# Branch C's projections spread between the attention units of the dilated heads

## The chip, the cores and the metric

The kernel runs on one core of one Trainium2 chip. The metric is the time of one execution in microseconds on the device. The kernel before takes 1748.67 us (median of 3 runs, 1744.22 to 1750.66). Engines are named as in the profile: PE is TensorE (PEld its weight loads), DVE is VectorE, ACT is ScalarE, POOL is GpSimd, SP is the engine that only issues DMAs here. All data is float32.

## The reference, cut to what matters

One layer for 512 prompt tokens and 8 x 8 sample tokens. The part that the change touches is the mixer:

```python
z = jnp.einsum('bld,de->ble', h, w_in)      # D_MODEL 1024
u, qb, kb, vb, qc, kc, vc, gl = jnp.split(z, cuts, axis=-1)
for g, (win, dil) in enumerate(((128, 1), (512, 4), (2048, 16))):
    o_g, l_g = dilated_prompt(qb[:, :, g], kb[:, :, g], vb[:, :, g], dil, bias_b[g])
oc, _ = band_attn(qc, kc, vc, bias_c, SWA_WINDOW, sink)   # branch C: 8 heads, 2 kv heads, 64 wide
y = merge(a, ob, lse, oc, gl, w_b_up, w_c_up, w_out)
```

`u` feeds the pooling branch, `qb, kb, vb` the 12 dilated heads (branch B), `qc, kc, vc` the 8 window heads (branch C). The dilated heads need nothing of branch C's projections. After the prompt's attention come the sample tokens' attention over cached keys, the merge, and the mixture of 64 experts, none of which is touched.

## The kernel before, in words

All engines run a fixed program, with semaphores between them. PE's results go through eight PSUM banks of 512 columns. A list of "fills", written by `plan()`, says in which order PE fills banks, which bank each fill takes (a ring over the banks), and whether ACT ("A") or DVE ("D") empties it. Before a fill PE waits until the fill that had its bank last has been emptied (`bank_for`). Each engine takes its work strictly in the order of its own code.

The projections: `by_channel` computes 128 channels x 288 tokens in 8 accumulated matmuls (`KD` = 8), `by_token` 128 tokens x 256 channels in 8. The order is u, q 0 to 5, k, v (branch B), and then branch C: q 6 to 9 in two halves each (8 fills of 8 matmuls with 288 moving columns) and kvc 0 to 4 (5 fills of 8 with 256). Two small fills `uout` (the last pooling rows, sent out by SP) follow, then the keys are turned: `kT` 0 to 6 (4 transposes each; 6 is branch C's key) and `kTs` (7 transposes of the sample tokens' keys).

Then the prompt's attention, 40 units in `UNITS`: 8 of the head group 1, 8 of group 2, 8 of group 0, 16 of branch C. A unit is two heads on one block of 128 queries. Units run in a software pipeline of 43 steps `s`: in step s PE makes the scores S of unit s (two matmuls; 128 columns each for the groups 1 and 2 and the first blocks, 256 for the others), turns the probabilities T of unit s - 2 (2 or 4 transposes), and multiplies with the values, O, for unit s - 3 (2 or 4 matmuls of 128 columns). For unit s DVE adds the bias and takes the maximum (L1700, L1704), ACT takes the exponential (L1274) and empties T (L1184), and DVE writes the outputs of unit s - 3 (L1652 to L1654). Queries of the groups 1 and 2 are read with a stride of four floats, as the stationary operand: `q = qT[rows, cq, t:SEQ:4]`.

Two waits stand in the pipeline. ACT waits before step 0 for `u_out`, the two DMAs of the pooling rows, whose staging place the scores take over. DVE waits at step 3 (`if s == LAGO`) for `kv_out`, all 28 DMAs that send keys and values out, because its `stage` array lies on the keys `kTM`. When the groups 1 and 2 are staged, SP writes them to `fold` in HBM and reads them back in token order; POOL and DVE combine the groups at step 30, and PE turns the result (`bT`) at step 37.

SP issues its DMAs in the order of its code: after the weights the bias tables, `u_out`, the keys and values out, then four loads of cached keys into the slots 3, 0, 1 and 2, then `fold`. A slot is 4096 floats per partition; a load waits until the slot's last reader on PE is done (`LAST`). POOL issues copies of the caches from HBM to HBM, one after each of the fills in `COPY_AT`.

Of the kernel before, what the change touches and what calls it, by code (L numbers as in the profile page):

```python
# [17 lines left out]
ACT = mybir.ActivationFunctionType  # L18
# [3 lines left out]
P = 128  # L22
# [37 lines left out]
def plan():  # L60
# [36 lines left out]
    for c in range(6, 10):  # L97
        for h in range(2):
            fill(("q", c, h), "AD"[h])
    for t in range(TILES):  # L100
        fill(("kvc", t), "AD"[t % 2])
    fill(("uout", 0), "A")
    fill(("uout", 1), "A")
    for m in range(7):
        fill(("kT", m), "AD"[m % 2])
    fill(("kTs",), "D")
# [94 lines left out]
LAGT, LAGO = 2, 3  # L201
COMBINE_AT = 27
# [151 lines left out]
def build(nc, x_prompt, x_sample, cache_b1, cache_b2, cache_b3, cache_c, state_pool, c_prompt, c_sample,  # L354
# [13 lines left out]
    with ExitStack() as ctx:  # L368
# [87 lines left out]
        stage = at(A_KTM, 3, PT_ * 264)  # L456
# [237 lines left out]
        def _(sp):  # L694
# [156 lines left out]
            for t in range(TILES):  # L851
# [3 lines left out]
                wait_emptied(sp, ("kvc", t))  # L855
                for kv, src in ((0, kTM), (1, vTM)):
# [4 lines left out]
                    if t == PT_ - 1:  # L861
                        sp.dma_start(b1_p[0, 0, :, kv, :, :].rearrange("i h d -> i (h d)"),
                                     src[:, t, 0:256]).then_inc(kv_out, 16)
                        sp.dma_start(c_p[0, 0, :, kv, :, :].rearrange("i h d -> i (h d)"),
                                     src[:, t, 768:896]).then_inc(kv_out, 16)
                    if t == PT_:

                        for o, n, w, c in [(outs_s[g], CACHE[g], 256, 256 * g) for g in range(3)] + [(c_s, P, 128, 768)]:
# [4 lines left out]
            for key in kload[:4]:  # L873
                load(key)
# [7 lines left out]
            for g in (1, 2):  # L882
                sp.dma_start(stage[:, g, :].rearrange("p (t c) -> p t c", t=PT_),
                             fold[g - 1].rearrange("(t p) c -> p t c", p=P)).then_inc(stage_in, 16)

# [286 lines left out]
        def _(act):  # L1172
# [61 lines left out]
            for c in range(6, 10):  # L1234

                bank = wait_fill(act, ("q", c, 0))
                for e in range(2):
                    h = 2 * (c - 6) + e
                    ins = act.activation(qT[64 * (h // 4):64 * (h // 4) + 64, 6 + h % 4, 0:288],
                                         bank[64 * e:64 * e + 64, 0:288], ACT.Copy)  # L1240
                ins.then_inc(emptied["A"], 1)
            for t in range(0, TILES, 2):
                r = parts(t)
                bank = wait_fill(act, ("kvc", t))
# [1492 lines left out]
```

## Time and profile before

| | us |
|---|---|
| median of 3 runs | 1748.67 (1744.22 to 1750.66) |
| the profiled execution | 1733.79, its span 1732.1 |
| PE busy | 1563.6 (90% of the span) |
| ACT busy | 509.6 |
| DVE busy | 474.7 |
| POOL busy | 264.9 |
| granted TensorE clock, mean | 0.928 |

A clock of 1.00 is 2.4 GHz, and 0.50 is 1.2 GHz. A float32 matmul of the program stands in the trace as two records of PE. Records overlap in the pipeline, so a record's mean duration is longer than the distance between starts; distances between starts, and busy time divided by the count, are the ones to add up. A PE that is busy by the trace is not PE at its peak.

### The profile page before, as it was taken

How to read it: one execution, taken by the hardware profiler on the slowest of the kernel's cores; microseconds unless marked ns; L12 is line 12 of the kernel's file. 1: busy time of each engine (PE TensorE's matmuls, PEld its weight loads, DVE VectorE, ACT ScalarE, POOL GpSimd, SP SyncE). 2: the span in 40 equal slices, each digit the busy share in tenths (PEclk: the TensorE clock that was granted, in tenths of full speed). 3: DMA queues.
4: the chain of work that ended last, by engine and by line, in shares of the span. 5: the costliest groups of instructions: out<-in, count | busy, mean ns of one | idle time of the engine just before them, and what ended most of it. 6: DMA issues, size and time to landing. Idle time of an engine off the chain costs nothing.

```text
span 1732.1 us, 22957 instructions
## 1 busy us (share of the span) xinstructions
PE 1563.6 (90%) x7181; PEld 881.1 (51%) x7182; DVE 474.7 (27%) x953; ACT 509.6 (29%) x854; POOL 264.9 (15%) x322
## 2 busy tenths in 40 slices
PE   4489999989897999997889879999999999999955
PEld 1057888877764777775345423333333333333311
DVE  2030000145672111111266422222222222212137
ACT  2110000045641000000233234444454444444321
POOL 0030051000300000000111112212122221211153
PEclk7689999966997999998989989999999999999988
DMA  8892379472388936549534299999879998999867
GB/s 289 302 337 26 50 235 331 163 241 64 131 279 257 302 94 203 178 160 329 207 123 169 85 364 393 345 383 411 325 275 342 405 420 341 420 417 422 321 266 249
DMA packets 140516, 461.29 MB, mean 266 GB/s; under 512 B 13401, under 2 KB 78425, under 8 KB 111308
## 3 DMA queue, kind: packets, MB, share of 16 engines
q1 hardware_dynamic: 117853, 331.36, 52.3%
q0 software_dynamic: 22608, 129.18, 21.1%
q8 instruction: 36, 0.59, 0.1%
q14 instruction: 19, 0.16, 0.0%
HBM read 424.80 MB, written 109.28 MB: 308 GB/s over the span
## 4 chain that ended last, share of the span: by engine, by line
PE 79%; DMA 7%; DVE 3%; SPq 3%; POOL 2%; issue 2%; ACT 2%; another core or an unknown queue 1%; ACTq 0%; POOLq 0%; DVEq 0%
PE bank L2107 72%; PE bank L2639 3%; POOL arena L1166 2%; DMA arena<-in_we_down 2%; SPq L783 1%; PE bank L2272 1%; DMA arena<-in_cache_b 1%; PE bank L2661 1%; PE bank L2313 1%; DMA arena<-in_w_in 1%; DMA arena<-in_w_ada 1%; DMA mods<-arena 1%; DMA arena<-in_we_gate 1%; DMA pscale<-in_pool_scale 1%
## 5 line engine op out<-in xcount | busy, mean ns | idle before, releaser
L2107 PE MATMUL bank<-arena 128*64 (+10 forms) x6096 | 1417.0, 513 | 118.4 <-DMA arena<-in_w_ada 26.5
L2107 PEld LDWEIGHTS bank<-arena 128*64 128x64 f32 (+3 forms) x6096 | 748.7, 173 | 680.9 <-issue 467.3
L1184 ACT ACTIVATE arena<-bank 128x512 f32<-128x512 f32 (+6 forms) x152 | 75.1, 505 | 350.5 <-PE bank L2107 219.8
L2026 DVE COPY arena<-bank 128x512 f32<-128x512 f32 x52 | 36.0, 692 | 409.0 <-PE bank L2639 409.0
L1441 ACT ACTIVATE arena<-arena 128x2048 f32 x52 | 99.7, 1918 | 19.5 <-DMA arena<-in_we_gate 15.7
L1128 POOL DMA_INDIRECT arena<-h2rows,icol x54 | 95.6, 1771 | 46.6 <-POOL icol L1124 46.6
L1450 ACT ACTIVATE arena<-arena 128x2048 f32 x52 | 99.3, 1910 | 11.4 <-issue 11.4
L1533 DVE COPY arena<-bank 128x512 f32<-128x512 f32 (+6 forms) x70 | 41.8, 606 | 209.7 <-PE bank L2107 185.8
L1460 ACT ACTIVATE arena<-bank 128x256 f32<-128x256 f32 x52 | 19.9, 383 | 239.5 <-PE bank L2107 239.5
L1323 ACT ACTIVATE arena<-bank 128x288 f32<-128x288 f32 x48 | 19.7, 410 | 233.6 <-PE bank L2107 233.6
L1085 POOL DMA_DIRECT2D out<-in_cache_b x24 | 12.0, 507 | 429.5 <-PE bank L2107 429.5
L2639 PEld LDWEIGHTS bank<-ident,arena 128*128 128x128 f32 x416 | 50.9, 194 | 44.6 <-issue 44.6
L2021 DVE COPY arena<-arena 128x2048 f32 x52 | 63.3, 1218 | 27.2 <-ACTq L1433 27.2
L1124 POOL COPY icol<-arena 128x1 uint32 (+1 forms) x54 | 9.6, 178 | 358.3 <-PE bank L2639 357.7
L2639 PE MATMUL bank<-ident,arena 128*128 128x128 f32 x416 | 60.9, 290 | 2.4 <-issue 2.4
L2041 DVE COPY arena<-bank 128x512 f32<-128x512 f32 x52 | 35.9, 691 | 80.4 <-PE bank L2107 80.4
L1844 DVE SCALAR_TENSOR_TENSOR arena<-bank,pscale,arena 128x288 f32<-128x288 f32 x16 | 8.3, 518 | 167.6 <-PE bank L2107 167.6
L1137 POOL DMA_DIRECT2D yrows<-arena x52 | 30.1, 579 | 131.1 <-DVE arena L2041 110.3
L1471 ACT ACTIVATE arena<-bank 128x512 f32<-128x512 f32 x52 | 31.0, 596 | 61.1 <-PE bank L2107 61.1
L1166 POOL DMA_INDIRECT arena<-yrows,arena x40 | 39.7, 993 | 15.1 <-issue 11.9
L1465 ACT ACTIVATE arena<-bank 128x512 f32<-128x512 f32 x52 | 31.0, 597 | 35.5 <-PE bank L2639 35.5
L2661 PEld LDWEIGHTS bank<-ident,arena 128*128 128x128 f32 x104 | 16.5, 207 | 42.7 <-issue 41.4
(235 smaller groups left out, 732.3 us busy)
## 6 DMA issues: line engine op xcount, KB each, us to landing
arena<-in_we_gate SPq DMA_DIRECT2D x64, 1024.0 KB, 11.2
arena<-in_we_up SPq DMA_DIRECT2D x64, 1024.0 KB, 13.6
arena<-in_we_down SPq DMA_DIRECT2D x64, 1024.0 KB, 11.0
out<-in_cache_b POOLq DMA_DIRECT2D x8, 4080.0 KB, 15.0
yrows<-arena POOLq DMA_DIRECT2D x52, 512.0 KB, 9.2
arena<-in_w_ada SPq DMA_DIRECT2D x12, 2048.0 KB, 16.7
arena<-in_cache_b SPq DMA_DIRECT2D x18, 1024.0 KB, 8.4
arena<-in_w_in SPq DMA_DIRECT2D x7, 2048.0 KB, 15.5
```

What stands on the lines that cost most here:

```text
L1128: pool.indirect_dma_start(xg[:, j, :], None, h2rows, bass.IndirectOffsetOnAxis(ap=icol[:, j:j + 1], axis=0), bounds_check=TOK - 1, oob_is_ ...
L1166: pool.indirect_dma_start(gbuf[n % GBUFS][0:r, :], None, yrows, bass.IndirectOffsetOnAxis(ap=rowi[0:r, TOPK * t + k:TOPK * t + k + 1], axis=0)
L1184: act.activation(out, pick(bank), ACT.Copy).then_inc(emptied["A"], 1)
L1441: act.activation(whalf[:, 2048:4096], arena[:, bass.ds(base + 2048, 2048)], ACT.Copy).then_inc(up_copied, 1)
L1450: act.activation(whalf[:, 4096:6144], arena[:, bass.ds(base + 4096, 2048)], ACT.Copy).then_inc(d_copied, 1)
L1533: dve.tensor_copy(out, pick(bank)).then_inc(emptied["D"], 1)
L2021: dve.tensor_copy(whalf[:, 0:2048], arena[:, bass.ds(base, 2048)]).then_inc(gate_copied, 1)
L2026: dve.tensor_copy(xT[:, 512:1024], psb[2][:, :]).then_inc(xt_dve, 1)
L2041: dve.tensor_copy(yb[:, off % 2, 512:1024], psb[5][:, :]).then_inc(y_dve, 1)
L2107: return pe.matmul(out, lhsT, rhs, start=first, stop=last)
L2639: ins = pe.transpose(psb[1 + k // 4][:, P * (k % 4):P * (k % 4 + 1)], xg[:, off % 2, k:D:KD], ident[:, :])
L2661: ins = pe.transpose(psb[3][:, k * P:(k + 1) * P], act3[:, 1, k:FF:2], ident[:, :])
```

## The change

Branch C's 13 projection fills (8 of q, 5 of kvc) leave their place ahead of `uout`. Their 104 matmuls are dealt out over the steps 0 to 20 of the attention pipeline, five per step: two behind the scores S, two behind the transposes T, one behind the products O. They use the banks 6 and 7 in turn; the other fills of the attention rotate over the banks 0 to 5. ACT empties the even ones, DVE the odd ones, at the same places of their own step. `kT` 6 and `kTs` move to the head of step 22 (`KEYS_AT`), and the first unit of branch C (step 24) waits for them.

`stage` moves from the keys' place to slot 3, so the wait for `kv_out` moves from step 3 to step 27, the first output of branch C. Slot 3's first cached-key load comes after the last `bT` fill, slot 2's after `kvc` 4 and behind `fold`, and branch C's keys and values go out behind `fold` as well.

```diff
+    ring["set"], ring["n"] = list(range(6)), 0
+
+    def between(s, place):
+        for x in beside(s, place):
+            if x % KD == KD - 1:
+                j = x // KD
+                fill(BESIDE[j], "AD"[j % 2], 6 + j % 2)
 
     for s in range(len(UNITS) + LAGO):
+        if s == KEYS_AT:
+            fill(("kT", 6), "A")
+            fill(("kTs",), "D")
         if s < len(UNITS):
             fill(("S", s), "D")
+        between(s, 0)
         if 0 <= s - LAGT < len(UNITS):
             fill(("T", s - LAGT), "A")
+        between(s, 1)
         if 0 <= s - LAGO < len(UNITS):
             fill(("O", s - LAGO), "D")
+        between(s, 2)
...
+BESIDE = [("q", c, h) for c in range(6, 10) for h in range(2)] + [("kvc", t) for t in range(TILES)]
+KEYS_AT = 22
+
+def beside(s, place):
+    lo, hi = ((0, 2), (2, 4), (4, 5))[place]
+    return range(5 * s + lo, min(5 * s + hi, KD * len(BESIDE)))
...
-        stage = at(A_KTM, 3, PT_ * 264)
+        stage = at(3 * SLOT, 3, PT_ * 264)
...
-            for key in kload[:4]:
+            for key in kload[1:3]:
                 load(key)
...
+            for t in (PT_ - 1, PT_):
+                wait_emptied(sp, ("kvc", t))
...
+            load(kload[3])
+            sp.wait_ge(fills_done, INDEX[("bT", PT_ - 1)] + 1)
+            load(kload[0])
...
-                if s == LAGO:
+                if s - LAGO == UNITS.index(("C", 0, 0)):
                     dve.wait_ge(kv_out, 16 * KV_OUTS)
...
+            def between(s, place):
+
+                for x in beside(s, place):
+                    j, k = divmod(x, KD)
+                    key = BESIDE[j]
+                    if k == 0:
+                        bank_for(pe, key)
+                    bank = psb[6 + j % 2]
+                    w = wait_load(pe, ("in", 5 if j < 4 else 6))
+                    if key[0] == "q":
+                        col = 256 + (key[1] - 6) * P if j < 4 else (key[1] - 8) * P
+                        ins = mm(bank[:, 0:288], w[:, 512 * k + col:512 * k + col + P],
+                                 hT[:, k, 288 * key[2]:288 * key[2] + 288], k == 0, k == KD - 1)
+                    else:
+                        ins = mm(bank[0:parts(key[1]), 0:256], hT[:, k, toks(key[1])],
+                                 w[:, 512 * k + 256:512 * k + 512], k == 0, k == KD - 1)
+                    if k == KD - 1:
+                        close(ins)
```

On PE, at the end of the projections and the head of the attention, the program stood as follows before (288 columns are q 6 to 9, 256 kvc, the 15- and 64-row ones `uout`, L2233 `kT`, L2237 `kTs`, then S of the units 0 to 2 and T of unit 0).

```order
L2107 MATMUL bank2<-arena 128x288 x8
L2107 MATMUL bank3<-arena 128x256 x8
...
L2107 MATMUL bank7<-arena 64x256 x8
L2219 MATMUL bank0<-ident,arena 15x128 x4
L2223 MATMUL bank1<-ident,arena 64x128 x4
L2233 MATMUL bank2<-ident,arena 128x128 x4
...
L2233 MATMUL bank0<-ident,arena 128x128 x4
L2237 MATMUL bank1<-ident,arena 128x64 x7
L2107 MATMUL bank2<-arena 128x128 x2
L2107 MATMUL bank3<-arena 128x128 x2
L2107 MATMUL bank4<-arena 128x128 x2
L2272 MATMUL bank5<-ident,arena 128x128 x2
```

The same engine and place now (L2294 is `kT`, L2344 T, L2156 all matmuls; the 288-column ones are q 6).

```order
L2283 MATMUL bank4<-ident,arena 64x128 x4
L2294 MATMUL bank5<-ident,arena 128x128 x4
...
L2294 MATMUL bank2<-ident,arena 128x128 x4
L2156 MATMUL bank0<-arena 128x128 x2
L2156 MATMUL bank6<-arena 128x288 x5
L2156 MATMUL bank1<-arena 128x128 x2
L2156 MATMUL bank6<-arena 128x288 x3
L2156 MATMUL bank7<-arena 128x288 x2
L2156 MATMUL bank2<-arena 128x128 x2
L2156 MATMUL bank7<-arena 128x288 x2
L2344 MATMUL bank3<-ident,arena 128x128 x2
```

Ahead of the first T, PE now has 12 projection matmuls besides the three units' scores. On SP, from the pooling rows to `fold`, the order is now this (L863, L864 the pooling rows, L874 to L882 keys and values out, L744 to L755 cached keys, L892 `fold`).

```order
L863 DMA out_6<-arena 15x512 [waits emptied_by_act]
L864 DMA out_11<-arena 8x8x512
L874 DMA out_3<-arena 128x256 [waits emptied_by_act]
...
L882 DMA out_9<-arena 8x8x256
L744 DMA arena<-in_cache_c 128x8x128 [waits fills_done]
L746 DMA arena<-in_cache_b1 128x8x256
L755 DMA arena<-in_cache_b3 128x8x256 [waits fills_done]
...
L892 DMA fold<-arena 128x264 [waits stage_ready]
```

Two of the four cached-key loads stand ahead of `fold` where all four did, and the other two behind it.

## Rows read from the trace of the kernel before

**Rows 1.** The page: busy time by engine; granted clock in 40 slices.
```profile
PE 1563.6 (90%) x7181; PEld 881.1 (51%) x7182; DVE 474.7 (27%) x953; ACT 509.6 (29%) x854; POOL 264.9 (15%) x322
...
PEclk7689999966997999998989989999999999999988
```

**Rows 2.** Stages from-to: length, busy time (records) of each engine, clock, DMA share, GB/s.
```profile
300.30:348.60 48.30, 48.30 (x209) 38.21 (x208) 4.62 (x12) 4.16 (x13) 0.00 (x0) 1.00 0.50 167
348.60:353.90 5.30, 4.58 (x43) 4.23 (x42) 2.70 (x4) 3.76 (x8) 0.00 (x0) 1.00 0.30 91
...
371.10:413.40 42.30, 42.30 (x149) 33.95 (x150) 21.29 (x79) 18.87 (x79) 0.00 (x0) 0.50 0.61 191
...
484.70:521.20 36.50, 35.87 (x322) 23.48 (x320) 25.96 (x50) 17.74 (x35) 0.00 (x0) 1.00 0.91 289
```

**Rows 3.** The same view in stretches of 5 us, where the clock moves.
```profile
355.00:360.00 5.00, 2.52 (x12) 2.03 (x10) 2.35 (x6) 3.72 (x13) 0.00 (x0) 0.63 0.79 263
...
415.00:420.00 5.00, 5.00 (x27) 4.39 (x28) 2.94 (x7) 2.08 (x6) 0.00 (x0) 0.73 0.41 147
```

**Rows 4.** PE in order of time: start, length, what [idle before, released by].
```profile
353.94 2.10 PE L2107 MATMUL bank<-arena 64*128 64x128 f32 x12 [0.77 <-DVE arena L1533]
358.52 0.66 PE L2272 MATMUL bank<-ident,arena 128*128 128x128 f32 x2 [2.48 <-ACT arena L1274]
...
371.08 0.66 PE L2272 MATMUL bank<-ident,arena 128*128 128x128 f32 x2 [2.58 <-DVE arena L1700]
...
373.75 0.69 PE L2272 MATMUL bank<-ident,arena 128*128 128x128 f32 x2
...
376.45 0.69 PE L2272 MATMUL bank<-ident,arena 128*128 128x128 f32 x2
...
414.91 1.11 PE L2272 MATMUL bank<-ident,arena 128*128 128x128 f32 x4
...
421.27 0.66 PE L2272 MATMUL bank<-ident,arena 128*128 128x128 f32 x4
...
423.39 0.66 PE L2272 MATMUL bank<-ident,arena 128*128 128x128 f32 x4
```

**Rows 5.** Matmul forms on PE, 301 to 349.4 us: records, busy us, mean ns.
```profile
L2107 PE MATMUL bank<-arena 128*128 128x288 f32 x125 | 30.5, 406 | 0.0
L2107 PE MATMUL bank<-arena 128*128 128x256 f32 x64 | 14.0, 379 | 0.0
```

**Rows 6.** The same, 205 to 245 us (stationary operand read with stride 4).
```profile
L2107 PE MATMUL bank<-arena 128*128 128x256 f32 x130 | 31.3, 401 | 0.0
```

**Rows 7.** DVE in order of time, at the wait of step 3.
```profile
368.51 0.17 DVE L1652 COPY arena<-nmx 128x2 f32<-128x2 f32 x1 [7.18 <-PE bank L2107]
```

**Rows 8.** Emptying half of q 6 to 9, 301 to 349 us, on DVE.
```profile
L1622 DVE COPY arena<-bank 64x288 f32<-64x288 f32 x8 | 3.6, 456 | 31.7 <-PE bank L2107 31.6
```

**Rows 9.** SP's and POOL's DMA issues and ACT's first exponential, in order of time.
```profile
350.70 0.71 SPq L848 DMA_DIRECT2D out<-arena  x1
...
406.16 4.75 SPq L879 DMA_DIRECT2D fold<-arena  x8
...
285.42 1.46 POOL L1085 DMA_DIRECT2D out<-in_cache_b  x3 [20.65 <-PE bank L2107]
...
356.20 1.28 ACT L1274 ACT_TABLE_LOAD   x1 [2.97 <-DVE nmx L1704]
```

**Rows 10.** DMA issues, KB each, us to landing: 285 to 326 us, then 200 to 500.
```profile
out<-in_cache_b POOLq DMA_DIRECT2D x1, 1008.0 KB, 39.3
...
arena<-in_cache_b SPq DMA_DIRECT2D x8, 1024.0 KB, 8.4
...
arena<-toep SPq DMA_DIRECT2D x12, 128.0 KB, 4.2
```

**Rows 11.** PE: `bT` and the first cached keys of group 2.
```profile
461.12 1.04 PE L2301 MATMUL bank<-ident,arena 128*128 128x128 f32 x8
...
490.50 1.97 PE L2313 MATMUL bank<-ident,arena 128*128 128x128 f32 x16
```

More of the change, by code:

```diff
@@ L1250, in _ @@
             act.wait_ge(tables_out, 16 * 8)
-            for m in range(0, 7, 2):
+            for m in range(0, 6, 2):
                 empty(("kT", m), kT[:, m, 0:SEQ])
@@ L1256, in _ @@
             for s in range(len(UNITS) + LAGO):
+                if s == KEYS_AT:
+                    empty(("kT", 6), kT[:, 6, 0:SEQ])
+                between(s, 0)
                 u = s - LAGT
@@ L1712, in _ @@
                     outputs(s - LAGO)
+                between(s, 2)
+                if 0 <= s - LAGO < len(UNITS):
                     if s - LAGO == COMBINE_AT:
@@ L2228, in _, with turned_own_keys @@
                     wait_emptied(pe, ("k", g, t))
-                wait_emptied(pe, ("kvc", t))
-            for m in range(7):
+            def turned_own_keys(m):
                 bank = bank_for(pe, ("kT", m))
@@ L2234, in _ @@
                 close(ins)
-            bank = bank_for(pe, ("kTs",))
-            for m in range(7):
-                ins = pe.transpose(bank[:, m * NS:(m + 1) * NS], kTM[0:NS, PT_, m * P:(m + 1) * P], ident[0:NS, 0:NS])
-            close(ins)
-            for m in range(7):
+            for m in range(6):
+                turned_own_keys(m)
+            for m in range(6):
                 wait_emptied(pe, ("kT", m))
@@ L2245, in _ @@
             for h in range(2):
-                wait_emptied(pe, ("q", 9, h))
+                wait_emptied(pe, ("q", 5, h))
             for s in range(len(UNITS) + LAGO):
+                if s == KEYS_AT:
+                    for t in range(TILES):
+                        wait_emptied(pe, ("kvc", t))
+                    turned_own_keys(6)
+                    bank = bank_for(pe, ("kTs",))
+                    for m in range(7):
+                        ins = pe.transpose(bank[:, m * NS:(m + 1) * NS], kTM[0:NS, PT_, m * P:(m + 1) * P],
+                                           ident[0:NS, 0:NS])
+                    close(ins)
                 if s < len(UNITS):
                     kind, t, p = UNITS[s]
+                    if (kind, t, p) == ("C", 0, 0):
+                        wait_emptied(pe, ("kT", 6))
+                        for h in range(2):
+                            wait_emptied(pe, ("q", 9, h))
                     bank = bank_for(pe, ("S", s))
@@ L2263, in _ @@
                     close(ins)
+                between(s, 0)
                 u = s - LAGT
@@ L2275, in _ @@
                     close(ins)
+                between(s, 1)
                 u = s - LAGO
@@ L2290, in _ @@
                     close(ins)
+                between(s, 2)
                 for key in after_unit(u):
```

91 lines of the change are left out of this document (49 added, 42 removed).

## The prediction

> **What bounds the kernel now.** I read the page first. PE is busy for 90% of the span, and its granted clock is low in a few slices [rows 1]. Slices 9 and 10 (346 to 433 us) read 6: the attention of the prompt. The stage view shows why it matters. From 300.3 to 348.6 us PE does branch C's projections at clock 1.00. From 371.1 to 413.4 us it is busy without a break at clock 0.50, while DVE works 21.3 of 42.3 us and ACT 18.9 [rows 2]. So in that stretch neither DVE nor ACT nor a DMA ends last: PE does, at 1.2 GHz. PE in order of time shows steps of 2.70 us (373.75 to 376.45) in the groups 1 and 2, and 2.12 us (421.27 to 423.39) for larger units once the clock is back [rows 4]. The clock fell between 355 and 360 us, when PE idled 0.77 and 2.48 us with a stretch of transposes just before, and rose between 415 and 420 us, when units with 256-column scores came [rows 3, 4]. Since all that follows is chained to the attention's end, a microsecond saved here is one off the span.
>
> **The old interval.** Everything compared lies between 300.3 us (first matmul of q 6) and the scores of step 21. T of step 21 starts at 414.9 [rows 4]; the 512 score columns ahead of it took about 1.7 us at the low clock, so step 21 began near 413.2. Old: 48.3 (projections) + 5.3 (`uout`, keys turned, up to 353.9) + 59.3 (steps 0 to 20) = 112.9 us. In the 59.3 lie two stalls of PE: 2.48 us for the first exponential and 2.58 us for the wait of step 3, at which DVE sat 7.18 us [rows 4, 7].
>
> **The new interval, if PE keeps its full clock.**
> - The 104 matmuls cost the same wherever they stand: 48.3 us. From the forms, two records of 288 columns take 0.488 us (30.5/62.5), that is 1.69 ns per column; of 256, 0.4375 us [rows 5].
> - The units' own work. A full-clock step of 2.12 us holds 1024 matmul columns (1.73 us at 1.69 ns) and 4 transposes, which leaves 0.10 us for each. Steps 0 to 20 hold 6144 columns of scores (18 units of 256, 3 of 512), 4608 of outputs (18 units) and 40 transposes: 10.4 + 7.8 + 3.9 = 22.1 us.
> - Scores of the groups 1 and 2 load a strided stationary operand. The projections that do so took 31.3/130 = 0.241 us a record against 14.0/64 = 0.219 [rows 5, 6], so 0.24 us looks like the price of one such load. A unit has four records: up to 0.96 us against 0.43 for its columns, with the first load behind a projection matmul. I take 0.4 us of excess for each of 16 units, 6.4 us; the ends are 0 and 8.5.
> - `uout` and 24 instead of 28 transposes, with the wait for the last copy: 5.3 less about 0.45 and 0.65 for what moved to step 22: 4.2 us. At step 22 that 1.1 us is paid again, now at the side of units at full clock.
> - DVE's and ACT's added emptying: DVE's halves are 0.456 us each [rows 8], two per fill, 6 fills in 21 steps; with 1.3 us of unit work a step (21.3 us in some 16 steps [rows 2]) DVE is at half of a 3.8 us step. ACT is lighter. Cost nothing; if a step were as short as before the change at full clock, they would show.
> - Stalls: the wait at step 3 is gone. Before the first T, PE now has 12 projection matmuls, 5.9 us, and three units' scores. `u_out` is issued near 302 us, into the shadow of POOL's third cache copy (issued 285.4, 39.3 us to landing, so until 324.7) [rows 9, 10]. Before it had landed within 5 us of its issue at 350.7 to 351.4, as ACT began at 356.2. T of unit 0 needs it by about 310. Small hardware-queue transfers landed in 4.2 us at the median [rows 10]. I take 1 us of stall, ends 0 and 14.
> - The clock's start: `kT` transposes and a gap of about 1 us come before step 0, as before. If it dips there, dense matmuls follow at once; I take 1 us, ends 0 and 4.
>
> New: 48.3 + 22.1 + 6.4 + 4.2 + 1 + 1 = 83.0 us, against 112.9: 29.9 us less. Behind it: the 1.1 us of step 22; six banks instead of eight for the branch C units, where DVE is the busier engine, 1 us (0 to 4); and T of the steps 21 and 22, which ran half slow (415 to 420 us at 0.73 [rows 3]), come at full clock, 2.1 us gained. Net 29.9 - 1.1 - 1 + 2.1 = 29.9, say **30 us**.
>
> What could be late next. `fold` takes 4.75 us to issue [rows 9] and some 4 to land, by the small transfers [rows 10]; then comes 1 us of issue for the read-back, and branch C's outputs, about 2 us to issue and 4 to land: 16 us in all. From step 18 (when it starts) to step 27 (where DVE now waits for `kv_out`) two mixed steps and seven of 2.12 us or more pass, 22 us: covered, with 6 us to spare. Slot 3's keys are now requested after `bT` (461.1), are two loads of 8.4 us to landing, 17 us even one after the other, and group 2's turn begins 29 us later (490.5) [rows 10, 11]: covered.
>
> **A rule weighed.** In the stretch from 484.7 to 521.2 us PE cycles through banks in short groups, many of them of transposes, and the clock stays at 1.00 [rows 2, 11]. The Trainium skill says the opposite of both habits: "TensorE: Matmul & The Clock Gate", section "A second HAM failure mode: psum-queue depth-cycling", has groups that cycle through banks with small gaps throw the clock back and forth, and its section "Part 4: PE-mode transpose" says that transposes do not count as busy. By these rules the half-clock rival below would be likelier than I make it; the trace disagrees once the clock is up, and agrees for 355 to 415 us.
>
> **The rivals.**
> - *The clock stays at 1.2 GHz through the mixed steps* (slower). PE in order cannot shed the added matmuls, so each costs double: 96.6 us, and the units what they cost before less the stalls, 59.3 - 5.1 = 54.2. With 4.2: 155.0 against 112.9, and 2.1 us behind: 44 us slower, **1793 us**. For it: 42 us of unbroken PE work at 0.50 did not lift the clock [rows 2]. Against it: a mixed step is two thirds full-height matmuls of 256 and 288 columns, which ran at 1.00 for the whole of 300 to 348 us, and thinner steps lifted it at 415 to 420 us. It decides from about 8 of the 21 steps on: a step at half clock costs some 3.7 us more, and the gain is 30.
> - *The units keep their 2.70 us* because the hand-over S, DVE, ACT, T, O sets it, and the projections only add: 48.3 + 54.2 + 4.2 = 106.7, 6 us less, with 2 behind 4: **1745 us**. Against it: DVE and ACT idle half the time in the old steps, and two steps lie between S and T.
> - *The new wait is `u_out`*: it lands only when the cache copy is through, at 324.7. PE stands for 14 us from about 310, and some 3 us more go into a cold clock: 30 - 17 + 1 + 1 = 15 us gained, **1734 us**. Against it: the bias tables, small and on the same hardware queue, landed in 4.2 us beside other loads [rows 10].
>
> The Trainium skill, "DMA: Bandwidth & Descriptors", section "Queues, rings and completion order", has each DMA engine take turns between its queues, packet by packet; by that, the third rival would not come.
>
> **How the numbers follow.** The trace is of an execution of 1733.8 us (span 1732.1 and 1.7 around it), 14.9 us under the median; 30 us off it are 1703.8, and off the median **1719 us**. I expect the median's offset to stay. The ends of the costs give a gain of 39 (no strided excess, no stall) to 20: 1710 to 1729 us; with the 3 us by which the three runs spread, 1706 to 1732. Chances: forecast 0.76, `u_out` 0.08, units' period 0.07, half clock 0.07, anything else 0.02. Up to 1736 the range holds the `u_out` rival too, and leaves out about 0.17. About 0.5% (9 us) is what can be told from no change here: faster by more is 0.86, within it 0.06, slower by more 0.08.
>
> **What would show it.** Right: clock 1.00 from 305 us to the end of the mixed steps; steps of 3.5 to 4 us, PE busy throughout; step 21 begins near 383; no idle time of DVE at step 3. Wrong: a clock of 0.50 beyond the first two or three steps; PE idle ahead of the first T with ACT waiting for the pooling rows; PE idle in the mixed steps, released by DVE or ACT; DVE standing at step 27; or PE waiting for slot 3's keys.

## The result, and the profile after

Beside the kernel before (1748.67 us) the changed kernel has a median of 1735.09 us over five executions (1730.67 to 1738.24): ratio 0.9922, 95% interval 0.99 to 0.9944, so 13.6 us faster (9.8 to 17.5), where 30 were forecast. Timed again later beside the kernel before (e13 below) it had 1737.85 against 1747.10, ratio 0.9961 (0.9935 to 0.9988). The mechanism came as forecast; its size was less than half.

The page after, busy time and granted clock as in [rows 1]:

```profile
PE 1560.6 (90%) x7181; PEld 873.6 (50%) x7182; DVE 476.3 (27%) x953; ACT 508.9 (29%) x854; POOL 268.3 (15%) x322
...
PEclk8589999999897999998989789999999999999987
```

Slices 9 and 10, which read 6, now read 9. PE's work is the same; it is done at the higher clock. By stages, with the columns of [rows 2] (from-to: length, busy time and records of PE, PEld, DVE, ACT, POOL, then clock, DMA share, GB/s): `uout` and keys; first scores to first T; T of unit 0 to T of unit 19 (made in step 21); and four stretches of 2 us in which the clock falls:

```profile
303.40:308.30 4.90, 3.64 (x34) 3.39 (x33) 2.08 (x3) 3.11 (x6) 0.00 (x0) 1.00 1.13 386
308.30:322.40 14.10, 11.50 (x36) 8.42 (x37) 2.53 (x6) 2.31 (x6) 0.00 (x0) 0.88 0.97 336
322.40:403.60 81.20, 81.20 (x373) 61.19 (x373) 29.37 (x102) 27.59 (x113) 0.00 (x0) 0.98 0.41 133
...
310.00:312.00 2.00, 2.00 (x6) 1.39 (x5) 0.45 (x2) 1.28 (x1) 0.00 (x0) 0.50 1.00 331
312.00:314.00 2.00, 2.00 (x7) 1.33 (x6) 0.00 (x0) 0.00 (x0) 0.00 (x0) 0.80 0.37 135
324.00:326.00 2.00, 2.00 (x6) 1.09 (x6) 0.00 (x0) 0.91 (x5) 0.00 (x0) 0.50 0.79 265
326.00:328.00 2.00, 2.00 (x10) 1.51 (x10) 1.34 (x4) 0.00 (x1) 0.00 (x0) 0.89 1.41 433
```

The stage of mixed steps is what the forecast wanted: busy 81.20 of 81.20 us, clock 0.98, DVE and ACT each at about a third. The clock dips twice, each time for some 3 us. PE in order of time (start, length, what, [idle before, released by]), which answers to [rows 4]:

```profile
303.37 0.61 PE L2279 MATMUL bank<-ident,arena 128*15 128x128 f32 x4
...
308.30 11.50 PE L2156 MATMUL bank<-arena 64*128 64x128 f32 x36 [1.26 <-DVE arena L1569]
322.40 0.41 PE L2344 MATMUL bank<-ident,arena 128*128 128x128 f32 x2 [2.60 <-ACT arena L1309]
322.65 5.09 PE L2156 MATMUL bank<-arena 128*128 128x288 f32 x14
...
336.41 0.38 PE L2344 MATMUL bank<-ident,arena 128*128 128x128 f32 x2
336.63 4.36 PE L2156 MATMUL bank<-arena 128*128 128x288 f32 x18
340.83 0.38 PE L2344 MATMUL bank<-ident,arena 128*128 128x128 f32 x2
...
403.56 0.66 PE L2344 MATMUL bank<-ident,arena 128*128 128x128 f32 x4
```

A mixed step takes 4.42 us (336.41 to 340.83). The T of step 21 (unit 19) stands at 403.56, before at 414.91 [rows 4]: the lead in this pair of traces is 11.4 us. The same view of SP and ACT shows what PE waited 2.60 us for:

```profile
305.17 0.37 SPq L863 DMA_DIRECT2D out<-arena  x1
305.58 0.70 SPq L864 DMA_DIRECT2D out<-arena  x1
306.53 24.34 SPq L874 DMA_DIRECT2D out<-arena  x10
...
310.56 1.28 ACT L1309 ACT_TABLE_LOAD   x1 [3.32 <-DVE nmx L1749]
321.38 0.40 ACT L1309 ACTIVATE arena<-arena,nmx 128x128 f32<-128x128 f32 x1 [9.54 <-DMA out<-arena]
```

SP issues the two writes of the pooling rows (`u_out`) by 306.28. ACT has its table at 311.8 and then stands until 321.38, released by those writes: 15 us from issue to landing. Before, with the issue at 350.70 to 351.41, ACT did not wait for them: its table load began at 356.20 [rows 9]. In the changed kernel this wait stands ahead of the first T.

Matmul forms on PE, 327 to 371 us (ten steps), which answer to [rows 5]:

```profile
L2156 PE MATMUL bank<-arena 128*128 128x288 f32 x98 | 29.6, 417 | 0.0
L2156 PE MATMUL bank<-arena 64*128 64x128 f32 x40 | 12.0, 419 | 0.0
L2156 PE MATMUL bank<-arena 128*128 128x128 f32 x40 | 6.1, 274 | 0.0
L2344 PE MATMUL bank<-ident,arena 128*128 128x128 f32 x20 | 3.8, 273 | 0.0
```

A unit has four records of scores (64 rows) and four of outputs (128 rows), of the same 128 columns. The outputs are busy 6.1 us, the scores 12.0. Here most of the forecast's error lies; a part of the difference, the strided read, it had in its sum.

### The profile page after: what moved, and what is told of

It reads as the page before. It is cut to its first block, busy times and chain, and to the rows that moved or that the text cites. A ratio compares the mean times of both kernels' runs of the same rounds, so it can differ in the third digit from the quotient of the medians.

```text
span 1733.5 us, 22973 instructions
## 1 busy us (share of the span) xinstructions
PE 1560.6 (90%) x7181; PEld 873.6 (50%) x7182; DVE 476.3 (27%) x953; ACT 508.9 (29%) x854; POOL 268.3 (15%) x322
## 4 chain that ended last, share of the span: by engine, by line
PE 78%; DMA 9%; DVE 3%; SPq 3%; issue 2%; ACT 2%; POOL 1%; another core or an unknown queue 1%; ACTq 0%; DVEq 0%; POOLq 0%
PE bank L2156 72%; PE bank L2713 3%; DMA arena<-in_we_down 3%; DMA arena<-in_w_ada 2%; SPq L799 1%; DMA arena<-in_cache_b 1%; DMA arena<-yrows,arena 1%; PE bank L2387 1%; POOL arena L1190 1%; PE bank L2735 1%; DMA out<-arena 1%; DMA mods<-arena 1%; PE bank L2344 1%; DMA pscale<-in_pool_scale 1%
## 5 line engine op out<-in xcount | busy, mean ns | idle before, releaser
L2156 PE MATMUL bank<-arena 128*64 (+11 forms) x6096 | 1420.4, 513 | 124.8 <-DMA arena<-in_w_ada 24.9
L2156 PEld LDWEIGHTS bank<-arena 128*64 128x64 f32 (+3 forms) x6096 | 741.6, 172 | 694.7 <-issue 478.5
L1486 ACT ACTIVATE arena<-arena 128x2048 f32 x52 | 99.3, 1910 | 11.4 <-issue 11.4
## 6 DMA issues: line engine op xcount, KB each, us to landing
arena<-in_we_down SPq DMA_DIRECT2D x64, 1024.0 KB, 11.4
```

The source lines that it names most:

```text
L1486: act.activation(whalf[:, 4096:6144], arena[:, bass.ds(base + 4096, 2048)], ACT.Copy).then_inc(d_copied, 1)
L2156: return pe.matmul(out, lhsT, rhs, start=first, stop=last)
```

## The experiments

Where a time is compared with another trace, the stretch meant is from the first scores (S of step 0) to T of unit 19, which step 21 makes: 95.3 us in the trace after, 96.4 in its second one (e13). The recorded expectations call its end "T of step 19".

| run | edit against the changed kernel | median us (executions) | ratio to before beside it (95%) | mixed step, us |
|---|---|---|---|---|
| e2, e16 | pooling rows staged elsewhere | 1723.50 (6), 1728.80 (4) | 0.9882 (0.9837-0.9928), 0.9883 (0.9817-0.9949) | 4.42 |
| e3 | scores read contiguously | 1725.21 (6) | 0.9885 (0.984-0.9931) | 3.93 |
| e4 | five projection matmuls in a row | 1729.86 (9) | 0.9916 (0.9891-0.9941) | 4.41 |
| e5 | nothing spread | 1747.28 (10) | 1.0019 (0.9994-1.0043) | 2.70, pure |
| e6 | e5 and e2 | 1743.64 (10) | 0.9993 (0.9964-1.0021) | 2.70, pure |
| e7 | e2, only two groups spread | 1727.24 (6) | 0.9892 (0.986-0.9924) | see text |
| e8 | e2, queries folded when emptied | 1717.50 (6) | 0.9848 (0.9819-0.9877) | 3.93 |
| e9 | e8, scores over 128 rows | 1710.04 (4) | 0.9807 (0.9771-0.9843) | 3.54 |
| e10 | fourth cache copy late | 1723.48 (4) | 0.9878 (0.983-0.9925) | 4.42 |
| e12 | e2, three matmuls a step | 1729.81 (6) | 0.9899 (0.9864-0.9934) | 3.28 |
| e13 | none | 1737.85 (12) | 0.9961 (0.9935-0.9988) | 4.42 |
| e14, e15 | two cache copies late | 1722.90 (4), 1728.68 (6) | 0.9861 (0.9809-0.9913), 0.9894 (0.9837-0.9952) | 4.42 |

**e1_before**: the kernel before, traced again.

> The kernel before, traced once more on the chip of the other runs. The traces before and after have nearly the same span (1732.1 and 1733.5 us), though the medians differ by 13.6 us. Theory A (the trace of before was a favourable execution: its granted clock happened to stay high from 920 to 990 us and at 465 us): this span comes out at 1742 to 1750 us, with less clock in stretches after the attention. Theory B (profiled executions of before are always faster than timed ones): again 1730 to 1735 us.

1738.61 us, span 1736.9: between the two ranges. Its steps are again 2.70 us and its stalls 2.48 and 2.55 us, so the stretch at half clock is a property of the kernel; the executions of the kernel before that were timed in that session lie between 1730.97 and 1753.76. A single execution says nothing about 10 us.

**e2_uout** and **e16_uout_again**: the rows wait elsewhere to be written out, and ACT no longer waits for them.

```diff
-        uouts = at(A_SC + 2 * UE + 4 * NS, 2, 512)
+        uouts = at(3072, 2, 512)
...
+            sp.wait_ge(u_out, 16 * U_OUTS)
             for key in [k for k in kload[4:5]] + [("V", "c0", 0)] + kload[5:]:
...
-            act.wait_ge(u_out, 16 * U_OUTS)
```

> The kernel after, with the pooling rows staged at the end of slot 0, where nothing is written until SP loads the second cached-key block, so ACT no longer waits for their two DMAs before the first exponential. Theory A (ACT's wait for u_out until 321 us cost PE the 2.6 us of idling, and the clock a second fall at 322 to 326 us): first exponential near 311 us, no idle time of PE before the first T, and 3 to 5 us off the kernel after (1730 us). Theory B (the clock falls anyway at the gap of 1.3 us before step 0, and PE ran slowly until 313): PE's idling goes, but the time to step 3 shrinks by 2.6 us or less.

> The changed kernel with the pooling rows staged elsewhere, so that ACT doesn't wait for their landing, timed and traced again beside the same kernel before. First it had 1723.5 us (ratio 0.9882) and 89.7 us from the first scores to T of step 19. Theory A: 1719 to 1727 us, ratio 0.984 to 0.989. Theory B: 1730 to 1735 us, ratio 0.990 to 0.993. Both expect no idle PE at the first T and 89 to 91 us.

PE in order of time, e2:

```profile
306.55 9.83 PE L2156 MATMUL bank<-arena 64*128 64x128 f32 x36 [1.29 <-DVE arena L1569]
316.22 0.38 PE L2344 MATMUL bank<-ident,arena 128*128 128x128 f32 x2
...
320.19 0.38 PE L2344 MATMUL bank<-ident,arena 128*128 128x128 f32 x2
```

No idle time before the first T, which comes 9.67 us after the first scores instead of 14.1, and the first step takes 3.97 instead of 5.18 us. The stretch is 89.6 us in both traces, 5.6 less than after. e16's median (1728.80) lies between the ranges of its two theories, its ratio (0.9883) in the first's; the ten executions have a mean of 1725.0 us.

**e3_nostride**: the scores of the groups 1 and 2 read contiguous query columns (the wrong tokens; the same amount of work).

```diff
-                        q = qT[rows, cq, t:SEQ:4] if kind in (1, 2) else qT[rows, cq, toks(t)]
+                        q = qT[rows, cq, toks(t)]
```

> The kernel after, with the queries of the groups 1 and 2 read as 128 neighbouring tokens instead of every fourth (the scores of these groups are then those of other queries). Mixed steps took 4.42 us against a forecast of 3.84. Theory A (the strided stationary operand costs 0.5 us a step, as the two units of group 0 with 128 columns suggest: 3.66 against 4.15 us): steps of 3.9 us, 16 x 0.5 = 8 us off. Theory B (the step is long because of the hand-overs between small groups): steps of 4.3 us or more.

PE in order of time, e3:

```profile
330.06 0.38 PE L2344 MATMUL bank<-ident,arena 128*128 128x128 f32 x2
330.28 3.87 PE L2156 MATMUL bank<-arena 128*128 128x288 f32 x18
333.99 0.38 PE L2344 MATMUL bank<-ident,arena 128*128 128x128 f32 x2
```

3.93 us a step: the strided load costs 0.49 us a unit. In this trace PE stood 9.31 us ahead of the first T, again released by ACT: the wait for the pooling rows varies.

**e4_grouped**: the five projection matmuls of a step in one place.

```diff
-    lo, hi = ((0, 2), (2, 4), (4, 5))[place]
+    lo, hi = ((0, 5), (5, 5), (5, 5))[place]
```

> The kernel after, with all five projection matmuls of a step behind the scores, instead of two, two and one behind S, T and O. Theory A (each change between a unit's short matmuls and the projections exposes a weight load of about 0.15 us): 4 changes a step fewer, steps of 4.42 - 0.4 = 4.0 us, 6 to 8 us off. Theory B (only the strided loads cost): steps stay at 4.4 us.

4.41 us a step against 4.42: taking the projections in one place instead of three saves nothing. The first theory fell; the 0.4 us too many in every step had to come from the units' own matmuls. From T of unit 1 to T of unit 19 it took 73.7 us against 76.0. Three matmuls (1.4 us) more stand ahead of that stretch here; the other 0.9 us falls in the last group's steps. Its stationary operand is 64 columns wide, and in the changed kernel it changes form at each of its places; that this change is the cause is argued, not shown.

**e5_none** and **e6_uout_none**: all thirteen groups of branch C ahead of `uout`, as before, in the banks 6 and 7, and all else as in the changed kernel; e6 adds e2's edit.

```diff
+NPRE = 13
...
+    if s < 0:
+        return range(KD * NPRE)
...
+            between(-1, 0)
```

> The kernel after with all 13 projection fills back ahead of the pooling rows (still in the banks 6 and 7); stage in slot 3, the moved waits, six banks and the late keys stay. It is the change without the spreading. Theory A (the spreading gives the gain, by the clock): the clock falls before the first T as before, steps of 2.70 us, no wait at step 3, so 3 to 5 us off the kernel before and 6 to 12 us slower than the change. Theory B (the moved wait gives most of it): as fast as the change, about 1733 us.

> As e5, and the pooling rows staged in slot 0 as in e2, so that neither stall is left. Theory A (the clock falls in any gap behind transposes, and PE still waits 2.5 us for the first exponential's table load): clock 0.50 from before step 2, steps of 2.70 us. Theory B (the two stalls brought the clock down): clock 1.00 throughout, steps of about 2.0 us, 12 us or more off e5.

PE in order of time, e5:

```profile
359.76 0.66 PE L2355 MATMUL bank<-ident,arena 128*128 128x128 f32 x2 [2.48 <-ACT arena L1318]
...
364.29 0.69 PE L2355 MATMUL bank<-ident,arena 128*128 128x128 f32 x2
364.77 2.29 PE L2166 MATMUL bank<-arena 128*128 128x128 f32 x8
366.99 0.69 PE L2355 MATMUL bank<-ident,arena 128*128 128x128 f32 x2
```

PE in order of time, and by stages, e6:

```profile
360.49 0.66 PE L2355 MATMUL bank<-ident,arena 128*128 128x128 f32 x2 [1.14 <-ACT arena L1318]
...
360.00:370.00 10.00, 9.51 (x35) 7.87 (x36) 4.79 (x18) 5.74 (x26) 0.00 (x0) 0.50 0.59 182
```

The stall at step 3 is gone, the wait for `kv_out` is later, the bank split is the new one, and nothing is gained (ratio 1.0019 and 0.9993), not even the 3 to 5 us that the first theory gave to the moved wait: the steps stand at 2.70 us again. The gain is the spreading alone. In e6 PE is idle for only 1.26 us ahead of the first scores and 1.14 ahead of the first T, and the clock is at 0.50 from 360 us on all the same. As these two short stalls remain, e6 shows that shorter stalls don't keep the clock, and not what happens with none.

**e7_uout_few2** and **e11_few2_again** (the same kernel): e2, with eleven groups ahead and the last two spread over the steps 0 to 3 (the lines are against e6's kernel).

```diff
-NPRE = 13
+NPRE = 11
```

> As e2, but only the last two fills (16 matmuls) are spread, over the steps 0 to 3; eleven stand ahead. Theory A (the clock needs something to keep it only across the first gap; the old steps were long only by the clock): clock 1.00 up to step 21 with steps of 1.9 to 2.1 us in the groups 1 and 2 (0.87 us of columns, 0.2 of transposes, 0.5 for the stride, some 0.4 of exposed weight loads), total within 3 us of e2. Theory B (thin steps let the clock fall by themselves): it falls after step 3 and steps are 2.70 us again, 15 us slower than e2.

> The kernel of e7 traced once more: its traced execution took 1749.8 us and the others 1715 to 1734. Theory A (where the thin steps lose the clock is chance): the clock falls at another step or not at all, and the span is 10 us or more shorter. Theory B (the thin steps lose it at the same place each time): 0.50 from step 6 again and about 1745 us.

PE in order of time, e7:

```profile
362.14 0.44 PE L2355 MATMUL bank<-ident,arena 128*128 128x128 f32 x2
...
364.08 0.44 PE L2355 MATMUL bank<-ident,arena 128*128 128x128 f32 x2
...
366.03 0.63 PE L2355 MATMUL bank<-ident,arena 128*128 128x128 f32 x2
...
368.67 0.69 PE L2355 MATMUL bank<-ident,arena 128*128 128x128 f32 x2
```

And its clock in stretches:

```profile
360.00:365.00 5.00, 5.00 (x26) 3.75 (x24) 2.05 (x7) 2.15 (x10) 0.00 (x0) 1.00 0.68 198
365.00:370.00 5.00, 5.00 (x20) 4.34 (x20) 2.56 (x11) 2.61 (x12) 0.00 (x0) 0.61 1.10 355
370.00:375.00 5.00, 5.00 (x20) 4.19 (x20) 2.50 (x10) 1.89 (x10) 0.00 (x0) 0.50 0.70 224
```

A pure step at full clock takes 1.94 us. In this trace the clock falls to 0.50 after the last mixed step although PE hasn't been idle for an instant, and the step becomes 2.70 us; e11's trace does the same at the same place (clock 0.61 at 370 to 375 us). So in these two executions, of 1749.76 and 1746.72 us, the pure steps lost the clock without a stall.

They are the two longest of this kernel's seven, and the others speak against making a rule of them. The five that weren't traced took 1715.45 to 1734.07 us, with a mean of 1725.8 and a mean clock over the whole execution of 0.933 to 0.944. The ten of e2 and e16, with all thirteen groups spread, have a mean of 1725.0 us and a clock of 0.937 to 0.946; e6's ten, with none spread, 1744.1 us and 0.918 to 0.929. Two groups over four steps thus gave the time that thirteen gave, as the first theory said of the total. That the clock held in those five is likely by these numbers, but no trace shows it. Whether the pure steps or the stalls ahead of them cost the old kernel its clock stays open.

**e8_foldq_uout**: e2, and the queries of the groups 1 and 2 are written in folded order when their banks are emptied, so that all scores are read contiguously. This computes all of the reference.

```diff
+                    empty(("q", c, 0), qT[:, c, 0:SEQ].rearrange("p (r i) -> p i r", r=4)[:, 0:72, :],
+                          lambda b: b[:, 0:288].rearrange("p (i r) -> p i r", r=4))
...
-                        q = qT[rows, cq, t:SEQ:4] if kind in (1, 2) else qT[rows, cq, toks(t)]
+                        q = qT[rows, cq, toks(t)]
```

> As e2, and the queries of the groups 1 and 2 are written in folded order when their banks are emptied (strided writes on ACT and DVE, one more DVE copy for each of four fills), so the scores read them without a stride. It computes all of the reference. Theory A (the stride costs 0.49 us a step, the writes are hidden behind PE): mixed steps of 3.93 us, 7.8 us off e2, about 1716 us. Theory B (the strided writes make ACT or DVE late in the projections): PE idle during q 2 to 5.

The step is 3.93 us, as in e3, and the emptying with a stride costs nothing that shows. At 1717.50 us (1718.0 in the mean, against 1725.0 of e2 and e16) it is the fastest kernel that does the whole work, 26 us under the kernel before beside it.

**e9_fullheight**: e8, and the scores contract over all 128 rows instead of one head's 64. Each score is then the sum of two heads, so this kernel doesn't compute the reference; it only prices the height.

```diff
-                        rows = slice(half, half + 64)
+                        rows = slice(0, P)
```

> As e8, but the scores take all 128 rows of queries and keys instead of the 64 of their head (each score is then the sum of two heads). Same columns, same number of weight loads. In e8's mixed step of 3.93 us the single records show 0.10 us extra before and 0.10 behind the first record at each change from a 128-row operand to a 64-row one and back, 0.39 us in all. Theory A (the change of height costs 0.2 us each way, because the next weights aren't loaded ahead): steps of 3.54 us, and 16 us less over the 40 units where PE is what ends last. Theory B (it is the semaphore wait ahead of the scores that holds the load back): steps stay at 3.9 us.

PE in order of time, e9:

```profile
329.47 0.38 PE L2354 MATMUL bank<-ident,arena 128*128 128x128 f32 x2
329.69 3.48 PE L2166 MATMUL bank<-arena 128*128 128x288 f32 x18
333.01 0.38 PE L2354 MATMUL bank<-ident,arena 128*128 128x128 f32 x2
...
391.62 0.60 PE L2354 MATMUL bank<-ident,arena 128*128 128x128 f32 x4
392.05 1.50 PE L2166 MATMUL bank<-arena 128*128 128x128 f32 x12
393.39 0.38 PE L2354 MATMUL bank<-ident,arena 128*128 128x128 f32 x2
```

With as many records and columns the step falls from 3.93 to 3.54 us, and a later pure step from 2.12 to 1.77. The 0.39 us is the price of going from 128 rows to 64 and back; the wait for a semaphore ahead of the scores is still there, so the second theory fell. The whole gained less than the 16 us expected: the mean of the executions fell from 1718.0 to 1711.3 us. In the single records of the trace after, the load ahead of a unit's first scores starts 385 ns after the load before it has ended, and the first full-height record behind them takes 0.35 us to the next start instead of 0.24: about 0.2 us each way. The Trainium skill ("TensorE: Matmul & The Clock Gate", section "Step-by-step: what each phase is for") says that a load is pulled ahead of matmuls in flight where the row groups don't conflict or where it goes to the background weight buffer, and that its time goes by the columns and not by the rows. Within one height the trace agrees: records of 128 columns start every 0.11 us. At each change of height the load wasn't ahead; which of the page's two conditions was missing there no run shows.

**e10_copy_late**, **e14_two_copies_late** and **e15_two_late_again**: POOL's fourth cache copy put off; then the third and the fourth.

```diff
-        COPY_AT = [("k", 0, 0), ("k", 2, 0), ("v", 0, 0), ("v", 2, 0), ("S", 30), ...
+        COPY_AT = [("k", 0, 0), ("k", 2, 0), ("S", 12), ("S", 20), ("S", 30), ...
```

> The kernel after, with POOL's fourth cache copy started after the scores of unit 16 instead of after the first value fill of group 2. Theory A (the pooling rows' DMAs landed 15 us after their issue because that copy filled the DMA engines): ACT's wait for them ends within 5 us of the issue, no idle time of PE before the first T, as in e2. Theory B (they are late for another reason, as SP's own queue): ACT waits until about 321 us again.

> The changed kernel with the third and the fourth cache copy of POOL put off: issued when the scores of the steps 12 and 20 are done, instead of when a value projection of group 0 and one of group 2 are. With the fourth alone put off the pooling rows, issued at 305.0 to 306.2 us, still landed only at 320.3, ACT standing 8.6 us. Theory A, these small writes wait behind the copies under way, three of which were issued together at 263 to 270 us: with two copies only, they land within 5 us of their issue, ACT's first exponential follows its table load (about 312 us), the first T comes at 313 to 314 us without an idle PE, the clock stays 1.00, and the time is 3 to 6 us under the changed kernel's. Theory B, the copies aren't it (it is the queue of SP's own transfers, or the form of the writes): ACT waits until about 320 us as before, no gain. The put-off copies run beside other work; on their account I expect nothing.

> The kernel with two cache copies put off, timed and traced again. In its one trace T of step 19 comes 3.9 us earlier after the first projection of branch C's successor stage than in the changed kernel's two traces (first scores to T of step 19: 91.3 us against 95.3 and 96.4), yet four executions have a median 15 us under the changed kernel's in the same session (1722.9 against 1737.9). Theory A, the 15 us are real: median 1719 to 1727 us and ratio 0.984 to 0.989 again, and a trace of an execution at that time shows a second stretch, outside 300 to 420 us, where it is shorter than the changed kernel's by some 10 us. Theory B, four executions are few: median 1730 to 1735 us, ratio 0.990 to 0.993, 4 us under the changed kernel.

ACT in order of time, e10 and then e14:

```profile
320.32 0.40 ACT L1309 ACTIVATE arena<-arena,nmx 128x128 f32<-128x128 f32 x1 [8.61 <-DMA out<-arena]
```

```profile
310.64 1.28 ACT L1309 ACT_TABLE_LOAD   x1 [3.33 <-DVE nmx L1749]
311.93 0.40 ACT L1309 ACTIVATE arena<-arena,nmx 128x128 f32<-128x128 f32 x1
```

SP in order of time, e14:

```profile
305.65 0.70 SPq L864 DMA_DIRECT2D out<-arena  x1
306.61 8.52 SPq L874 DMA_DIRECT2D out<-arena  x14
```

With the fourth copy alone put off, ACT still waited for the rows until 320.3. With the third put off too, they had landed when ACT's table was there, 5.6 us after the last issue, PE had no idle time at the first T, and SP needed 8.5 us to issue fourteen key and value writes where it had needed 24.3 for ten. So it is the cache copies under way, but not the one that my rival named (issued at 288.94 in the trace after, at 285.42 before [rows 9]).

The landing times in the traces say which. The copies land one after another: in the trace after the first three, issued from 262.80 to 267.90, had wholly landed at 282.0, 299.5 and 318.5 us, the fourth at 334.4. ACT went on at 321.38, behind the third and well ahead of the fourth; in e13 at 320.72 (third copy 319.7), in e10 at 320.32 (320.1). e3 fits less well (third 313.5, fourth 330.0, ACT 324.09). In e14 the last copy under way had landed at 291.8, ahead of the rows' issue, so there the rows met no copy at all.

e14's clock dipped even so (0.68 at 308 to 312 us), e15's didn't; the stretch took 91.3 and 89.6 us. e15's median and ratio lie between what its two theories said, and its trace has no other stretch that is 10 us shorter. The ten executions of the two have a mean of 1726.1 us.

**e12_rate3**: e2, with six groups ahead and seven spread at three matmuls a step.

```diff
+NPRE = 6
...
-    lo, hi = ((0, 2), (2, 4), (4, 5))[place]
+    lo, hi = ((0, 1), (1, 2), (2, 3))[place]
```

> As e2, but six fills stand ahead and the other seven are spread at three matmuls a step, over the steps 0 to 18. By e7 and e2 a unit's step costs 1.95 us at full clock and a projection matmul 0.49 on top, wherever it stands. Theory A (three matmuls a step still keep the clock): steps of 1.95 + 1.46 = 3.41 us at clock 1.00, total within 3 us of e2. Theory B (a step must be more than half projections): the clock falls, steps of about 5.6 us.

Clock by stretches, e12:

```profile
330.00:335.00 5.00, 5.00 (x15) 3.51 (x15) 1.15 (x3) 0.88 (x4) 0.00 (x0) 0.64 0.88 300
335.00:340.00 5.00, 5.00 (x16) 3.34 (x16) 1.38 (x4) 0.98 (x5) 0.00 (x0) 0.68 0.58 184
...
350.00:385.00 35.00, 35.00 (x173) 28.17 (x171) 15.30 (x60) 13.25 (x59) 0.00 (x0) 1.00 0.11 36
```

In this trace three matmuls a step hold the clock as well as five do, after a dip at the start: 3.28 to 3.45 us a step, where 3.41 was expected.

**e13_after_again**: the changed kernel, timed and traced again.

> The changed kernel, timed again in five rounds beside the kernel before, and traced again. Open is how much of the miss (30 us forecast, 13.6 measured) lies in the steps and how much is scatter of the executions. Theory A, a part is scatter: from the first 288-column matmul to the first scores of the sample units the two traces of before took 369.6 and 372.6 us, the trace of the changed kernel 353.1, so 18 us less; and two near relatives of it (fourth copy late, projections grouped) were timed at 1723.5 and 1729.9 beside a before of 1744. Then the ratio comes out at 0.988 to 0.991, 1723 to 1728 us, a gain of 16 to 21 us, and the stretch takes 353 us again. Theory B, the 13.6 us are what it gives: ratio 0.992 to 0.995, 1730 to 1735 us. Either way the trace shows steps of 4.42 us and ACT waiting until about 321 us for the pooling rows.

Neither theory: the gain beside the kernel before is 6.8 us (2.1 to 11.4) by the ratio, less than both. All 17 executions of the changed kernel have a mean of 1738.1 us (standard error 1.1), 78 of the kernel before in the later sessions 1745.0 (0.6): 7 us. The 13.6 us of the first comparison rest on five executions of each: the median of before was 3.7 us above that mean, the changed kernel's 3.0 below its own. The trace of e13 has the same steps, and ACT waited until 320.72; PE stood 3.26 us at the first T. But from the first 288-column matmul to the sample units' first scores it took 359.9 us, not 353 again.

## Why the prediction was wrong

**What held.** The old interval was read rightly: 42 us at half clock, bound by PE (e1 shows it again, e5 brings back its steps). The clock came to 1.00 in the mixed steps and stayed; the projection matmuls cost what they did (single records start every 0.243 us, as 30.5 us over 125 records said [rows 5]) and added to the units' work; PE never stood in the mixed steps; DVE's stall at step 3 went; no wait came at step 27 or for slot 3's keys. The rivals of half clock and of the units' own period were rightly low.

**The step that failed is the new interval, in its terms for the units.** From `uout` to the start of step 21 the forecast had 83.0 us; the trace has 99.3 (303.37 to about 402.7, as T at 403.56). The 16.3 us too many, by runs (in each row the excess is measured less forecast):

| term | forecast | measured | from |
|---|---|---|---|
| 64-row scores beside 128-row matmuls | nothing | 8.2 (21 steps by 0.39) | e9 |
| the first T, its wait and cold clock | 2 | 5.6 | e2 against after |
| strided load | 6.4 | 7.8 (16 by 0.49) | e3, e8 |
| `uout` to first scores | 4.2 | 4.9 | trace after |
| last group, 64 columns wide | nothing | about 0.9 | e4 |
| not split | | 1.5 | |

The first row is half of it, and it was there to be read. I took a full-clock step of 2.12 us for 1024 matmul columns at 1.69 ns (1.73 us) and left 0.39 us to four transposes, 0.10 each [rows 4]. But the scores in that stretch belong to branch C's first block, 256 columns and not 512. 768 columns are 1.30 us, the transposes 0.43, and 0.39 us is left over. It had been booked as columns, and so it vanished for the steps 0 to 20, whose columns I counted rightly. Had I divided each form's busy time by its records, the 64-row ones would have stood out.

The second row is my `u_out` rival at a third of its price: given 0.08, it came in both traces of the changed kernel, with 2.6 and 3.3 us idle (1.7, 4.0 and 9.3 in e10, e4 and e3) instead of 14. The argument against it, small loads landing in 4.2 us [rows 10], came from the bias tables, which SP asked for from 236.5 to 253.2 us, before POOL's first copy (257.25) was issued: they had no copy beside them. The prediction cited the Trainium skill ("DMA: Bandwidth & Descriptors", section "Queues, rings and completion order") for queues that take turns. The same section says further on that a transfer's semaphore is written only after every earlier write of its DMA engine, across the queues. I had read past that. The 15 us from issue to landing, ending just behind the third copy, and under 6 us with no copy under way, agree with it. But the fourth copy, issued 16 us ahead of the rows, didn't hold them until it had landed, and no run separates this rule from engines that were merely busy with the third copy.

The same miss can be read from the old state. By [rows 4] a pure step is 2.70 us at half clock, and I expected full clock to halve most of it. It is 1.94 (e7), so there were only 0.76 us a step to be had (what the loads and changes of form cost doesn't seem to halve with the clock, which no run takes apart): some 14 us over 19 steps, and 5 us of stalls, less 5.6 us for the new one, is 14 us, close to the 13.6 that the interval lost. The sum of 83.0 us asked for 30.

**What the interval gave the whole.** The interval is 13.6 us shorter (112.9 less 99.3), yet the executions gain 7 us over all of them and 14 in the first comparison. From the first 288-column matmul of the projections on, the two traces of before reach the experts after 884.5 and 889.6 us, those of the changed kernel after 879.2 and 880.1, 7.4 less in the mean; of a lead of 14.6 us at the sample units' first scores 2.4 were gone at the merge of the branches, 1.2 more at the output projection, and 3.6 more at the experts. From the output projection to the experts the traces of all kernels take either 166 to 168 us or 172 to 174, with a clock at 900 to 960 us of 0.94 to 1.00 in before (both), e8, e13, e14 and e16 and of 0.89 to 0.91 in after, e2 and e15; with two traces of a kernel nothing says that the earlier start has a part in it. Nor is it settled why the executions without the pooling rows' wait (means 1725.0 and 1726.1) lie 12 to 13 us under the changed kernel's, when their traces are 4 to 7 us shorter in the stretch and 6 in the span (1722.7, 1728.0, 1732.7 and 1727.1 against 1733.5 and 1733.8). The wait itself can't be all of it: e10 and e4 still have it in their traces, and their means are 1724.6 (4 executions) and 1730.2 (9). That the changed kernel is faster than the kernel before, and by some 7 us, is shown; the rest may lie in executions that weren't traced.

The range reached up to 1736 us only because of that rival. The likeliest case's own bounds (1710 to 1729) left the 14 us end of the stall to the rival and had no term for the 64-row scores.

## What to carry to other kernels

A stretch of thin matmuls that runs at half clock can be brought to full clock by putting dense ones of other work into its steps, even though PE has no idle time to fill: five a step did it, and three. Fewer may do: two groups at the head alone gave the same time in the executions that weren't traced (e7), and lost the clock in both that were. Price it by forms, with busy time over records for each height and width, since what a form costs beyond its columns has to be paid at full clock too. A wait that was harmless behind 48 us of other work (here for two small writes) is to be re-read at its new place against the copies that are under way there. And a stationary operand that is read with a stride is best written contiguously where the emptying engine has time: that gave another 7 us (e8), as much as the whole change by the mean of all its executions. Full height would be worth about as much again by e9, but a kernel that has it and still computes the right scores was not tried.

## What the runs showed of the chip that I had not expected

- The clock can fall without any gap on PE: busy throughout at 1.00, then two pure steps of 64-row scores, transposes and 128-column outputs, and it goes to 0.50 (e7, e11, the two traced executions). With three projection matmuls a step it stayed at 1.00 from 350 to 385 us (e12).
- Half clock costs a thin step 39%, not 100%: 2.70 against 1.94 us (e7).
- A change of the stationary operand from 128 to 64 rows and back costs 0.39 us, each 64-row unit again (e9: 3.54 against 3.93 us a step). Dealing the projections to one place instead of three changed a step by 0.01 us (e4).
- A stationary operand read with a stride of four f32 (every 16 bytes) costs 0.234 us from one record's start to the next, where a contiguous one costs 0.11, both beyond the change of height: 0.49 us a unit (e3, e8).
- Two writes of 30 and 128 KB took 15 us to land while a copy of 5.5 MB was under way that had been issued 37 us earlier, and under 6 when none was (trace after, e14).
